# One transformer encoder layer on eight cores: the first loads put in another order, with two waits

## The chip, the cores and the metric

The kernel runs on the 8 cores of one Trainium2 chip, each core on one batch element. The metric is the device time of the slowest core, in microseconds (us); lower is better. Below, PE or TensorE is the matmul engine, DVE or VectorE, ACT or ScalarE and POOL or GpSimd are the three others that compute, and SP only issues DMAs.

## The reference, cut to what matters

```python
def hybrid_layer(x, mem, ...):                       # x (8, 2048, 1024) f32
    proj = x @ w_in                                  # 5376 columns
    glu_in, q, k, v, q_mem, gate_logits = split(proj)
    y_conv = conformer_conv(glu_in, ...)             # a * sigmoid(g), depthwise conv of 31, LayerNorm, silu, @ w_conv_out
    y_attn = windowed_gqa(q, k, v, rel_bias, attn_sink) @ w_attn_out     # +-128 tokens, T5 bias, sink per head
    y_mem = memory_attention(q_mem, mem, w_mem_kv) @ w_mem_out
    gates = sigmoid(gate_logits + b_gate)
    merged = gates[0] * y_conv + gates[1] * y_attn + gates[2] * y_mem
    x = layer_norm(ALPHA * x + merged @ w_o)
    gate, up = split(x @ w_ffn_in)
    return layer_norm(ALPHA * x + (silu(gate) * up) @ w_ffn_out)
```

## The kernel before

Each core computes the whole layer for its 2048 tokens. The tokens are cut into four tiles of 512 (k = 0 to 3), and the GLU's 512 channels into four chunks (c = 0 to 3) with a gate half and an "a" half. One GLU group is eight matmuls of 128x128 by 128x512 into one PSUM bank. The program is one long list of instructions for each engine, written out in the order in which the Python code calls them; nothing reorders them at run time. Each engine runs its own list in order and stops at a wait.

Loads of weights and of x go out on GpSimd's queue (`load`, line 281), since they cast f32 to bf16 on the way; each has a semaphore of its own. Small constants go out on SP's queue, with one semaphore for rb33 and onehot (`t_rb`) and one for the five others, relvalid, bgate, dwsc, cvec and esink8 (`t_small`, line 279), which counts as reached when all five are there. `load_glu(c, half)` loads one block of GLU weights (128x1024; half 1 is the gate), `load_xt(k)` the two halves of x tile k (128x2048 each). In all eight blocks and two x tiles are issued at the start; then GpSimd sets up constants (identity, eps, masks, ones, pads; lines 302 to 318).

Around the start, the lists of the other engines are these:

- TensorE: gate group (tile 0, chunk 0), its first four matmuls on the first x half and the last four on the second; the "a" group of the same; the bias matmul on rb33 and onehot (`setup_bias`, line 449); gate (0, 1); a (0, 1); then the groups of tile 1 and the other chunks, sixteen groups in all. After them come the q groups, which need w_q.
- PSUM: groups of one bank take turns on four single banks (4 to 7). A bank comes free when the instruction that reads it is done: the tanh for a gate group, the multiply on VectorE for an "a" group, the exponential for the bias.
- ScalarE: first the exponential of esink8 (line 329), which waits for `t_small`; then the tanh of the first gate group (line 372), the exponential of the bias (line 452), and the other tanhs. A table load goes ahead of the first.
- VectorE: copies of the identity, two small scalings that wait for `t_small` (lines 325 and 327), the GLU multiply (line 380), the bias times relvalid (line 454).
- SP, behind its small loads: the store of the first GLU result to u_scratch, the store of the bias table to gexp_scratch, more stores of GLU results.
- GpSimd, behind its constants: the load of Brev from gexp_scratch, which waits for that store to land, and only then w_q, w_kv, w_qm, memt, w_mkv and x tiles 2 and 3.

```python
        for kc in range(8):
            tk = mm(ps[:, b, :], lhs(kc), rhs(kc), kc == 0, kc == 7,
                    [dd, deps, t_xt[k][0]] if kc == 0 else [t_xt[k][kc // 4]], inc=(kc == 7))
...
    t_esink = act.run(lambda: nc.scalar.activation(esink8[:], esink8[:], AF.Exp), [t_small])
...
        btab["st"] = load(gexp_d.ap(), geb, [t_b1], sp)
        btab["rev"] = load(Brev, bass.AP(gexp_d, 0, [[1, 128], [512, 8], [1, 384]]), [btab["st"]])
```

Of the kernel before, what the change touches and what calls it, by code (L numbers as in the profile page):

```python
# [93 lines left out]
def build_nc():  # L94
    plan = _build(None)[1]
    return _build(plan)[0]

def _build(plan):
    nc = bass.Bass("TRN2", target_bir_lowering=False)

    def din(name, shape):
        return nc.dram_tensor(name, list(shape), F32, kind="ExternalInput").ap()
# [5 lines left out]
    sinkp_d = din("sinkp", [1, 8])  # L108
    onehot_d = din("onehot", [32, 512])
    relvalid_d = din("relvalid", [1, 512])  # L110
    bgate_d = din("bgate", [128, 24])
    dwsc_d = din("dwsc", [128, 128])
    cvec_d = din("cvec", [128, 12])
# [21 lines left out]
    pool = Eng(nc, nc.gpsimd, "pool", plan)  # L135
    sp = Eng(nc, nc.sync, "sp", plan)
# [4 lines left out]
    def new_slot(name="s"):  # L141
        _slot_n[0] += 1
        return Slot(nc, f"{name}{_slot_n[0]}")

    def dma(e, out, in_, slot, deps=()):
        e.wait(deps)
        e.eng.dma_start(out=out, in_=in_).then_inc(slot.sem, 16)  # L147
        slot.count += 16
        return slot.tok()
# [3 lines left out]
    def V(kb, shape, dt=BF16, p0=0):  # L153
        esz = 2 if dt == BF16 else 4
        n = 1
        for s in shape[1:]:
            n *= s
        off = int(round(kb * KB))
        a = ARENA[p0:p0 + shape[0], off // 2: off // 2 + (n * esz) // 2]
        if dt != BF16:  # L160
            a = a.bitcast(dt)
        if len(shape) >= 3:
            names = "abcdefg"[:len(shape) - 1]
            pat = "p (" + " ".join(names) + ") -> p " + " ".join(names)
            a = a.rearrange(pat, **{nm: shape[i + 1] for i, nm in enumerate(names[:-1])})
        return a
# [4 lines left out]
    bgate = nc.alloc_sbuf_tensor("bgate_sb", [128, 24], F32)  # L171
    dwsc = nc.alloc_sbuf_tensor("dwsc_sb", [128, 128], F32)
    ident4 = nc.alloc_sbuf_tensor("ident4", [128, 32], F32)
    cvec = nc.alloc_sbuf_tensor("cvec_sb", [128, 12], F32)
    esink8 = nc.alloc_sbuf_tensor("esink8", [128, 8], F32)
# [91 lines left out]
    rv = V(145, [8, 512], F32)  # L267
# [4 lines left out]
    s_bias, s_small = new_slot("bias"), new_slot("small")  # L272
    dma(sp, rb33[:], rbp_d, s_bias)
    t_rb = dma(sp, oh, onehot_d, s_bias)
    dma(sp, rv, relvalid_d.partition_broadcast(8).rearrange("p a b -> p (a b)"), s_small)
    dma(sp, bgate[:], bgate_d, s_small)
    dma(sp, dwsc[:], dwsc_d, s_small)
    dma(sp, cvec[:], cvec_d, s_small)
    t_small = dma(sp, esink8[:], sinkp_d.partition_broadcast(128).rearrange("p a b -> p (a b)"), s_small)

    def load(out, in_, deps=(), e=None, name="ld"):
        return dma(e or pool, out, in_, new_slot(name), deps)

    t_glu, t_xt = {}, [[None] * 2 for _ in range(4)]

    def load_glu(c, half=None):
        for i in ((1, 0) if half is None else (half,)):
            t_glu[c, i] = load(wglu[:, c, i], w_glu_d[:, c, i])

    def load_xt(k):  # L290
        for h in range(2):
            t_xt[k][h] = load(xT[:, k, 4 * h:4 * h + 4, :], xt_d[:, k, 4 * h:4 * h + 4, :])

    load_glu(0, 1)
    load_xt(0)
    load_glu(0, 0)
    load_glu(1)
    load_xt(1)
    load_glu(2)
    load_glu(3)  # L300

    t_idz = pool.run(lambda: nc.gpsimd.memset(ident_f[:], 0.0))
    t_identf = pool.run(lambda: nc.gpsimd.affine_select(
        out=ident_f[:], in_=ident_f[:], pattern=[[-1, 128]], compare_op=ALU.not_equal,
# [11 lines left out]
    t_pads = pool.run(lambda: nc.gpsimd.memset(U0[:, :, T + 32:UW], 0.0))  # L316
    t_vones = pool.run(lambda: nc.gpsimd.memset(vaug[:, :, :, 64:65], 1.0))
    t_vm1 = pool.run(lambda: nc.gpsimd.memset(vm129[:, :, :, 128:129], 1.0))

    t_ident = dve.run(lambda: nc.vector.tensor_copy(ident_bf[:], ident_f[:]), [t_identf])  # L320
    for r in range(4):
# [1333 lines left out]
```

How the kernel before makes its waits and increments, by code:

```python
    def wait(self, deps):  # L45
        for tok in _flat(deps):
            if tok[0] == "E":
                _, src, v = tok
                k = id(src)
                if self.seen.get(k, 0) >= v:
                    continue
                self.seen[k] = v
                src.needed.add(v)
                if self.plan is not None:
                    self.eng.wait_ge(src.sem, src.vmap[v])
            else:
                sem, val = tok
                k = id(sem)
                if self.seen.get(k, 0) >= val:
                    continue
                self.eng.wait_ge(sem, val)
                self.seen[k] = val
# [1 line left out]
    def run(self, fn, deps=(), inc=True):  # L64
        self.wait(deps)
        ins = fn()
        if inc:
            self.v += 1
            if self.plan is None or self.v in self.plan[self.name]:
                ins.then_inc(self.sem, 1)
                self.real += 1
                self.vmap[self.v] = self.real
            return ("E", self, self.v)
        return None
# [70 lines left out]
    def dma(e, out, in_, slot, deps=()):  # L145
        e.wait(deps)
        e.eng.dma_start(out=out, in_=in_).then_inc(slot.sem, 16)
        slot.count += 16
        return slot.tok()
```

## Time and profile before

| | |
|---|---|
| time, median of 3 runs | 977.96 us (977.52 to 982.31) |
| the profiled execution's own time | 978.9 us |
| its span, first to last instruction, slowest core (7) | 977.9 us |
| spans of the eight cores | 970.8 to 977.9 us |
| busy on that core: PE, DVE, ACT, POOL | 96%, 63%, 45%, 30% |

The profile shows one execution. Its span runs from the first to the last instruction of the slowest core, and all times of a row count from the start of that span. "Idle before" is what an engine stood still just ahead of an instruction, and the arrow names what ended it. For a DMA the issue (on an engine's queue, SPq or POOL) and the landing are two different times.

### The profile page before, as it was taken

Reading aid. Unit: us, or ns where it says so; the run is one execution under the profiler, and the core shown is the slowest. Engines: PE = TensorE matmul, PEld = TensorE weight load, DVE = VectorE, ACT = ScalarE, POOL = GpSimd, SP = SyncE. Lnnn points to the kernel's source line nnn. Section 1 sums busy time; section 2 is a strip of 40 time slices with the busy share of each in tenths; the row PEclk is TensorE's granted clock in tenths of the full one; section 3 lists DMA queues with packets and bytes.
Section 4 is the critical chain, followed back from the end, with each engine's and each line's share of the span. In section 5 each row is a group of like instructions: output and inputs, shape, how many; then the busy total and the mean of one; then the engine's idle time right before and its main releaser. Section 6 shows DMA issues by size and latency. Waiting matters only on the chain.

```text
span 977.9 us, 16532 instructions; the slowest of 8 cores (970.8 to 977.9 us)
## 1 busy us (share of the span) xinstructions
PE 941.3 (96%) x5556; PEld 441.9 (45%) x5556; DVE 613.6 (63%) x997; ACT 438.9 (45%) x709; POOL 291.7 (30%) x296
## 2 busy tenths in 40 slices
PE   3999999999999999999999999999999999999997
PEld 1454544554444444444445444444444444444444
DVE  0323476667766857566668798876476666663555
ACT  1125657576663354444544455554122444443212
POOL 3200000112135334334321344444433233334331
PEclk9999999999999999999999999999999999999999
DMA  8898023374258999512486365665433323220232
GB/s 131 153 178 165 24 77 101 64 149 72 45 86 121 117 150 132 76 65 57 95 252 266 87 166 148 161 147 126 158 129 129 108 86 109 86 87 1 86 108 87
DMA packets 39683, 112.12 MB, mean 115 GB/s; under 512 B 4976, under 2 KB 16888, under 8 KB 38608
## 3 DMA queue, kind: packets, MB, share of 16 engines
q0 software_dynamic: 11104, 41.16, 29.0%
q1 hardware_dynamic: 28496, 69.91, 22.3%
q8 instruction: 46, 0.75, 0.3%
q14 instruction: 37, 0.30, 0.1%
HBM read 132.49 MB, written 30.47 MB: 167 GB/s over the span
## 4 chain that ended last, share of the span: by engine, by line
PE 83%; DMA 6%; DVE 5%; issue 3%; ACT 3%; SPq 0%; DVEq 0%; POOL 0%; ACTq 0%; POOLq 0%
PE ps L233 81%; DMA esink<-sinkp 2%; DMA arena<-w_q 2%; DMA arena<-w_bf_cache 1%; DMA gexp_scratch<-arena 1%; ACT arena L597 1%; ACT arena L645 1%; PE ps L1270 1%; DVE arena L1318 1%; DVE arena L1206 1%; DVE arena L1202 0%; DVE arena L807 0%; SPq L147 0%; DVE arena L806 0%; DVE arena L590 0%
## 5 line engine op out<-in xcount | busy, mean ns | idle before, releaser
L233 PE MATMUL ps<-arena 128*128 128x512 bf16 (+5 forms) x5146 | 925.7, 357 | 28.3 <-DMA arena<-xt 16.3
L233 PEld LDWEIGHTS ps<-arena 128*128 128x128 bf16 (+1 forms) x5146 | 421.9, 98 | 515.1 <-issue 69.0
L1315 ACT COPY arena<-ps 128x512 f32<-128x512 f32 x132 | 76.6, 586 | 137.3 <-PE ps L233 137.2
L1325 POOL TENSOR_TENSOR arena<-arena 128x512 bf16<-128x512 f32 x66 | 89.2, 1351 | 151.9 <-DVE arena L1318 143.8
L1318 DVE TENSOR_TENSOR arena<-arena,ps 128x512 f32<-128x512 f32 x132 | 88.0, 684 | 40.3 <-PE ps L233 39.4
L940 POOL TENSOR_TENSOR arena<-arena 128x512 f32<-128x512 f32 (+1 forms) x48 | 63.9, 1339 | 104.2 <-DVE arena L931 104.2
L1184 ACT ACTIVATE arena<-arena 128x1024 bf16<-128x1024 f32 x31 | 32.7, 1056 | 80.7 <-DVE arena L1474 69.8
L931 DVE SCALAR_TENSOR_TENSOR arena<-arena,ps 128x512 f32<-128x512 f32 x72 | 49.2, 684 | 23.9 <-ACT arena L927 18.0
L147 POOL DMA_DIRECT2D arena<-w_g x21 | 11.3, 545 | 168.4 <-PE ps L233 167.2
L923 DVE TENSOR_TENSOR arena<-arena,ps 128x512 f32<-128x512 f32 x54 | 37.1, 686 | 35.2 <-ACT arena L920 19.7
L1206 DVE SCALAR_TENSOR_TENSOR arena<-arena,rs 128x1024 bf16<-128x1024 f32 (+2 forms) x33 | 56.5, 1716 | 1.6
L920 ACT COPY arena<-ps 128x512 f32<-128x512 f32 x54 | 31.6, 585 | 55.8 <-PE ps L233 55.8
L927 ACT ACTIVATE arena<-arena,bgate_sb 128x512 f32<-128x512 f32 x54 | 39.0, 723 | 31.6 <-DVE arena L923 31.6
L645 ACT ACTIVATE arena<-ps 128x1024 bf16<-128x1024 f32 x46 | 46.6, 1025 | 13.3 <-PE ps L233 13.0
L648 DVE TENSOR_TENSOR arena<-arena 128x1024 bf16<-128x1024 bf16 x46 | 34.0, 740 | 28.8 <-ACT arena L645 28.7
L807 DVE TENSOR_TENSOR arena<-arena 128x512 bf16<-128x512 bf16 x53 | 46.7, 881 | 5.5
L1211 POOL TENSOR_TENSOR arena<-arena 128x1024 f32<-128x1024 f32 x16 | 39.9, 2501 | 30.0 <-ACT arena L1210 30.0
L1321 ACT ACTIVATE arena<-arena 128x512 f32<-128x512 f32 x66 | 41.8, 633 | 3.3 <-DVE arena L1318 3.1
L1198 POOL TENSOR_TENSOR rs<-mvt,eps_t 128x1 f32<-128x1 f32 x32 | 21.2, 663 | 73.4 <-DVE mvt L1194 63.6
L1202 DVE SCALAR_TENSOR_TENSOR arena<-arena,mvt 128x1024 f32<-128x1024 f32 (+1 forms) x33 | 42.1, 1278 | 1.5 <-DVE mvt L1194 0.2
L806 DVE TENSOR_TENSOR arena<-arena 128x1024 bf16<-128x1024 bf16 x53 | 38.6, 729 | 5.5 <-DMA arena<-w_bf_cache 5.4
L1474 DVE SCALAR_TENSOR_TENSOR arena<-arena,ps 128x1024 f32<-128x1024 f32 x15 | 18.3, 1218 | 36.5 <-PE ps L233 29.2
(117 smaller groups left out, 552.3 us busy)
## 6 DMA issues: line engine op xcount, KB each, us to landing
arena<-w_bf_cache SPq DMA_DIRECT2D x44, 512.0 KB, 3.9
arena<-u_scratch SPq DMA_DIRECT2D x64, 135.0 KB, 3.2
arena<-x SPq DMA_DIRECT2D x16, 512.0 KB, 13.9
y_scratch<-arena SPq DMA_DIRECT2D x16, 512.0 KB, 4.3
arena<-y_scratch SPq DMA_DIRECT2D x16, 512.0 KB, 3.6
out<-arena SPq DMA_DIRECT2D x15, 512.0 KB, 2.6
arena<-w_f POOLq DMA_DIRECT2D x22, 256.0 KB, 5.0
arena<-w_g POOLq DMA_DIRECT2D x9, 512.0 KB, 18.5
```

What stands on the lines that cost most here:

```text
L233: return pe.run(lambda: nc.tensor.matmul(out, lhsT, rhs, start=start, stop=stop, skip_group_check=onto), deps, inc)
L645: t_p = act.run(lambda: nc.scalar.activation(flat, bank2(b), AF.Exp, scale=0.125), [tk, PTw_free[rp], btab["t"]])
L807: t2 = dve.run(lambda: nc.vector.tensor_tensor(out=S[:, 2, :], in0=B[:, 2, :], in1=S[:, 0, :], op=ALU.subtract), [t1])
L931: t_y = dve.run(lambda: nc.vector.scalar_tensor_tensor(out=buf, in0=buf, scalar=1.0, in1=ps[:, bk, :], op0=ALU.add, op1=ALU.mult), [tk, t_th])
L940: t = pool.run(lambda: nc.gpsimd.tensor_tensor(out=out, in0=acc, in1=buf, op=ALU.add), [t_acc, t_y])
L1202: return dve.run(lambda: nc.vector.scalar_tensor_tensor(out=buf, in0=buf, scalar=mvt[:, k % 4, 0:1], in1=tab, op0=ALU.subtract, op1=ALU.mu ...
L1206: return dve.run(lambda: nc.vector.scalar_tensor_tensor(out=dst, in0=buf, scalar=rs, in1=tab, op0=ALU.mult, op1=ALU.add), deps)
L1211: return pool.run(lambda: nc.gpsimd.tensor_tensor(out=buf, in0=buf, in1=tab, op=ALU.add), [t])
L1315: return act.run(lambda: nc.scalar.copy(buf, ps[:, b, :]), deps)
L1318: return dve.run(lambda: nc.vector.tensor_tensor(out=buf, in0=buf, in1=ps[:, b, :], op=ALU.add), deps)
L1321: return act.run(lambda: nc.scalar.activation(buf, src, AF.Silu), deps)
L1325: return pool.run(lambda: nc.gpsimd.tensor_tensor(out=dst, in0=up, in1=gate, op=ALU.mult), deps)
```

## The change

GpSimd issues the gate block of chunk 0 and the two halves of x tile 0, then sets up its constants, then waits until that block has landed, then issues the other seven blocks and x tile 1. SP issues rb33 and onehot as before, then waits until the first half of x tile 0 has landed, and issues its five other loads after that. No instruction of another engine is moved.

```diff
@@ -272,33 +272,28 @@
     s_bias, s_small = new_slot("bias"), new_slot("small")
     dma(sp, rb33[:], rbp_d, s_bias)
     t_rb = dma(sp, oh, onehot_d, s_bias)
+
+    def load(out, in_, deps=(), e=None, name="ld"):
+        return dma(e or pool, out, in_, new_slot(name), deps)
+
+    t_glu, t_xt = {}, [[None] * 2 for _ in range(4)]
+
+    def load_glu(c, half=None):
+        for i in ((1, 0) if half is None else (half,)):
+            t_glu[c, i] = load(wglu[:, c, i], w_glu_d[:, c, i])
+
+    def load_xt(k):
+        for h in range(2):
+            t_xt[k][h] = load(xT[:, k, 4 * h:4 * h + 4, :], xt_d[:, k, 4 * h:4 * h + 4, :])
+
+    load_glu(0, 1)
+    load_xt(0)
+    sp.wait([t_xt[0][0]])
     dma(sp, rv, relvalid_d.partition_broadcast(8).rearrange("p a b -> p (a b)"), s_small)
     dma(sp, bgate[:], bgate_d, s_small)
     dma(sp, dwsc[:], dwsc_d, s_small)
     dma(sp, cvec[:], cvec_d, s_small)
     t_small = dma(sp, esink8[:], sinkp_d.partition_broadcast(128).rearrange("p a b -> p (a b)"), s_small)
-
-    def load(out, in_, deps=(), e=None, name="ld"):
-        return dma(e or pool, out, in_, new_slot(name), deps)
-
-    t_glu, t_xt = {}, [[None] * 2 for _ in range(4)]
-
-    def load_glu(c, half=None):
-        for i in ((1, 0) if half is None else (half,)):
-            t_glu[c, i] = load(wglu[:, c, i], w_glu_d[:, c, i])
-
-    def load_xt(k):
-        for h in range(2):
-            t_xt[k][h] = load(xT[:, k, 4 * h:4 * h + 4, :], xt_d[:, k, 4 * h:4 * h + 4, :])
-
-    load_glu(0, 1)
-    load_xt(0)
-    load_glu(0, 0)
-    load_glu(1)
-    load_xt(1)
-    load_glu(2)
-    load_glu(3)
-
     t_idz = pool.run(lambda: nc.gpsimd.memset(ident_f[:], 0.0))
     t_identf = pool.run(lambda: nc.gpsimd.affine_select(
         out=ident_f[:], in_=ident_f[:], pattern=[[-1, 128]], compare_op=ALU.not_equal,
@@ -316,6 +311,13 @@
     t_pads = pool.run(lambda: nc.gpsimd.memset(U0[:, :, T + 32:UW], 0.0))
     t_vones = pool.run(lambda: nc.gpsimd.memset(vaug[:, :, :, 64:65], 1.0))
     t_vm1 = pool.run(lambda: nc.gpsimd.memset(vm129[:, :, :, 128:129], 1.0))
+
+    pool.wait([t_glu[0, 1]])
+    load_glu(0, 0)
+    load_glu(1)
+    load_xt(1)
+    load_glu(2)
+    load_glu(3)
 
     t_ident = dve.run(lambda: nc.vector.tensor_copy(ident_bf[:], ident_f[:]), [t_identf])
     for r in range(4):
```

On GpSimd the start of its list before (after four constants of the framework), where the names are the tiles written and read, and arena is the large SBUF buffer:

```order
L147 DMA arena<-w_glu 128x1024 [waits barrier_Pool_Activation_PE_DVE_SP_gather]
L147 DMA arena<-xt 128x2048 x2
L147 DMA arena<-w_glu 128x1024 x3
L147 DMA arena<-xt 128x2048 x2
L147 DMA arena<-w_glu 128x1024 x4
L302 MEMSET ident_f 128x128
L303 AFFINE_SELECT ident_f<-ident_f 128x128 [waits sem_pool]
```

And now, from the ninth of its constants on; dq_ld3 is the semaphore of the first block, dq_ld34 that of the gexp store:

```order
L309 MEMSET ones_bf 128x128
L310 MEMSET arena 128x4x32
L311 MEMSET arena 128x4x16
L312 MEMSET arena 128x32
L313 MEMSET arena 128x8
L147 DMA arena<-w_glu 128x1024 [waits dq_ld3]
L147 DMA arena<-w_glu 128x1024 x2
L147 DMA arena<-xt 128x2048 x2
L147 DMA arena<-w_glu 128x1024 x4
L147 DMA arena<-gexp_scratch 128x8x384 [waits dq_ld34]
```

The constants now stand behind the first block and x tile 0 and ahead of the seven other blocks and x tile 1; the first of these blocks carries a wait for the block issued first.

On SP the start of its list, where dq_ld4 is the semaphore of the first half of x tile 0:

```order
 L147 DMA rb<-rbp 32x8 [waits barrier_Pool_Activation_PE_DVE_SP_release]
 L147 DMA arena<-onehot 32x512
-L147 DMA arena<-relvalid 8x512
+L147 DMA arena<-relvalid 8x512 [waits dq_ld4]
 L147 DMA bgate_sb<-bgate 128x24
 L147 DMA dwsc_sb<-dwsc 128x128
```

Nothing is moved on SP; the third load carries a new wait, and the four loads and all stores behind it follow it.

## Rows read from the trace of the kernel before

**Rows 1.** The page's head and its busy times, slowest core:

```profile
span 977.9 us, 16532 instructions; the slowest of 8 cores (970.8 to 977.9 us)
...
PE 941.3 (96%) x5556; PEld 441.9 (45%) x5556; DVE 613.6 (63%) x997; ACT 438.9 (45%) x709; POOL 291.7 (30%) x296
```

**Rows 2.** Timeline, TensorE, core 7, 10 to 60 us: start, duration, engine, line, operation.

```profile
13.76 1.87 PE L233 MATMUL ps<-arena 128*128 128x512 bf16 x4 [13.76 <-DMA arena<-xt]
17.57 5.08 PE L233 MATMUL ps<-arena 128*128 128x512 bf16 x12 [1.95 <-DMA arena<-xt]
22.58 1.02 PE L233 MATMUL ps<-arena,rb 32*8 32x512 f32 x2
23.54 4.49 PE L233 MATMUL ps<-arena 128*128 128x512 bf16 x20
28.60 20.02 PE L233 MATMUL ps<-arena 128*128 128x512 bf16 x92 [0.57 <-DMA arena<-xt]
50.18 10.02 PE L233 MATMUL ps<-arena 128*128 128x512 bf16 x62 [1.56 <-DMA arena<-w_q]
```

**Rows 3.** Chain of waits in order of time, core 7: start, duration, what.

```profile
4.47 17.28 DMA esink<-sinkp
...
25.28 8.26 DMA gexp_scratch<-arena
...
35.05 14.99 DMA arena<-w_q
```

**Rows 4.** DMA view, 10 to 14 us: queue, packets, MB, share of 16 engines.

```profile
q0 software_dynamic: 169, 0.53, 88.9%
q1 hardware_dynamic: 169, 0.05, 9.1%
```

**Rows 5.** DMA view, 14 to 18 us.

```profile
q0 software_dynamic: 283, 0.54, 92.1%
q1 hardware_dynamic: 255, 0.02, 7.9%
```

**Rows 6.** DMA view, 4 to 18 us.

```profile
q0 software_dynamic: 715, 1.84, 93.6%
q1 hardware_dynamic: 567, 0.10, 6.9%
```

**Rows 7.** DMA view, 18 to 32 us.

```profile
q0 software_dynamic: 920, 2.19, 99.8%
```

**Rows 8.** Timeline, SP's queue and GpSimd, core 7, 0 to 26 us.

```profile
1.98 0.48 SPq L147 DMA_DIRECT2D arena<-relvalid  x1
...
4.47 1.27 SPq L147 DMA_DIRECT2D esink<-sinkp  x1
...
7.99 0.32 POOL L302 MEMSET ident_f<- 128x128 f32 x1
...
10.40 0.20 POOL L318 MEMSET arena<- 128x8 bf16 x1
```

**Rows 9.** DMA issues by line, 0 to 60 us: queue, KB, us to landing.

```profile
rb<-rbp SPq DMA_DIRECT2D x1, 1.0 KB, 1.5
```

**Rows 10.** Timeline, ScalarE, core 7, 20 to 36 us.

```profile
21.83 1.28 ACT L329 ACT_TABLE_LOAD   x1 [21.83 <-DMA esink<-sinkp]
...
23.24 0.58 ACT L372 ACTIVATE arena<-ps 128x512 f32<-128x512 f32 x1
```

**Rows 11.** Tile w_glu, 0 to 60 us (all eight), then its first load alone.

```profile
L147 POOL DMA_DIRECT2D arena<-w_glu x8: 557/606/733, 1.5 to 7.5; - x8
...
DMA to landing us min/median/max: 7.5/22.1/28.7
...
DMA to landing us min/median/max: 7.5/7.5/7.5
```

**Rows 12.** Busy time by window; the third last column is PEclk, the granted clock.

```profile
17.50:22.60 5.10, 5.03 (x13) 1.63 (x14) 0.26 (x2) 0.77 (x1) 0.00 (x0) 1.00 1.05 175
```

**Rows 13.** Timeline, TensorE, core 3, from x tile 1 on.

```profile
28.68 20.02 PE L233 MATMUL ps<-arena 128*128 128x512 bf16 x92 [2.25 <-DMA arena<-xt]
```

More of the change, by code:

```diff
@@ L274, in _build @@
     t_rb = dma(sp, oh, onehot_d, s_bias)
[L275 to L279, printed above, removed]
     def load(out, in_, deps=(), e=None, name="ld"):
@@ L295, in _build @@
     load_xt(0)
-    load_glu(0, 0)
-    load_glu(1)
-    load_xt(1)
-    load_glu(2)
-    load_glu(3)
+    sp.wait([t_xt[0][0]])
+    dma(sp, rv, relvalid_d.partition_broadcast(8).rearrange("p a b -> p (a b)"), s_small)
+    dma(sp, bgate[:], bgate_d, s_small)
+    dma(sp, dwsc[:], dwsc_d, s_small)
+    dma(sp, cvec[:], cvec_d, s_small)
+    t_small = dma(sp, esink8[:], sinkp_d.partition_broadcast(128).rearrange("p a b -> p (a b)"), s_small)
     t_idz = pool.run(lambda: nc.gpsimd.memset(ident_f[:], 0.0))
```

## Prediction

> **What bounds the kernel now.** Read the page's head first: TensorE is busy for 941.3 of 977.9 us [rows 1]. Whatever this change does, it does to the few stretches in which TensorE stands still. They lie at the start. The timeline of TensorE on core 7, the slowest, shows them [rows 2]: 13.76 us until the first half of x tile 0 is there, 1.95 until the second half, 0.57 for x tile 1, and 1.56 before 50.18 for w_q. In between, sixteen groups of eight matmuls (GLU, x tiles 0 and 1) are run without another wait. Past 50.18 TensorE is nearly always busy, so I take a shift of that point to pass whole into the end.
>
> Next, the chain of waits says why w_q is late [rows 3]. It starts with esink, the last small load of SP: issued at 4.47, landed 17.28 us later. ScalarE's first instruction waits for it; behind it come the tanh of the first gate group, the exponential of the bias, the store of gexp (25.28, 8.26 us to land), and only then may GpSimd issue the load of Brev and of w_q (35.05, 14.99 us to land). So the small loads that the change delays are the head of the chain that sets 50.18. That is the first thing to hold on to.
>
> Third, the DMA view by window shows why such small loads take so long. From 10 to 14 us GpSimd's queue q0 and SP's queue q1 each moved 169 packets [rows 4], from 14 to 18 us 283 and 255 [rows 5]: they take turns, one packet for one packet, though q1's are worth only 8 to 9% of the time. A small packet waits for a large one.
>
> **The change part by part** (times of core 7 in the profiled execution).
>
> *SP's five loads wait for the first x half.* They no longer share the engines while x tile 0 comes in. From 4 to 18 us q0 moved 1.84 MB [rows 6]; from 18 to 32 us, nearly alone, 2.19 MB [rows 7]. At the second rate the first would take 0.84 of its time. Upper bound of the gain: 16% of the 9.8 us from 4 to 13.76, 1.6 us; lower bound: q1's own 6.9% share, 0.7 us. Middle: 1.2 us, so the first half lands at about 12.6. For the second half (17.57, so 13.6 us) the same working gives 0.9 to 2.2, middle 1.6: 16.0.
>
> *The five loads land later.* The first was issued at 1.98, the last 2.5 us after it [rows 8]; now 12.6 and 15.1. Bounds for how long they then need: q1 put 567 packets through from 4 to 18 us [rows 6]; at the 64 per us of 14 to 18 us (beside w_glu's small packets) that is 8.9 us, at the 42 of 10 to 14 us (beside x's large ones) 13.4. Add 1.5 us from issue to a small load's landing in a free queue [rows 9]: 23.0 to 27.5. The far end: as long as before, 21.8 less 1.98, 19.8 us, so 32.4. The stream behind x tile 0 is now three w_glu blocks, then x tile 1, so between the two rates, 25.3; since the last ones trailed before (they landed at 21.8, not at 18), I take 26.0, against 21.8.
>
> *Who waits for them.* ScalarE waits at its first instruction, and all its work is queued behind it. From the wake at 21.83 to the end of the first tanh (23.24 plus 0.58) are 2.0 us [rows 10]; so the tanh ends at 28.0. TensorE has four single PSUM banks; two groups, the bias matmul and the second gate group fill them, and the next group (a, chunk 1) reuses the bank that this tanh frees. Before, that group began at 23.54 plus eight matmuls of 0.2245, 25.3, with the tanh done at 23.8: no wait. Now TensorE would be ready 7.8 us after the second half, at 23.8, and has to wait until 28.0: **a new stall of 4.2 us**, which the trace of before has nowhere. From that group to the end of the sixteen are 48.62 less 25.34 less the 0.57 that now is hidden, 22.7 us: 50.7 instead of 48.6.
>
> *The gexp store and w_q.* The store is issued 4.2 us later too, at 29.5. It landed in 8.26 us beside x tile 1's large packets. Bounds: 1.5 us (rows 9's small load) and 8.26; q0's last w_glu block is through at 7.5 plus 28.7, 36.2 us [rows 11], so nothing of q0 holds the store much past that. I take 6.0, near the upper end, since there is still a stream: 35.5, 2.0 us later than before. Brev and w_q follow at once: w_q at 52.0, TensorE's q groups at 52.2 instead of 50.18.
>
> *GpSimd's constants and its wait.* The constants (2.6 us, from 7.99 on [rows 8]) run while the x halves come in; nobody needs them before 23 us. The first block landed 7.5 us after its issue at 1.55 [rows 11], so GpSimd goes on at about 9.1; queued behind the wait are all further blocks, x tile 1, and later Brev and w_q. The x halves keep the engines fed until 16.0, so a block issued at 9.1 starts in time. I cost it at nothing; were that cover gone (first block past 13 us), each us would come straight on top.
>
> **Sum:** the x tile earlier by 1.6, the tanh later by 4.2, TensorE past its last early wait at 52.2 instead of 50.2: **2.0 us slower**. The profiled execution took 978.9 us, 1.0 more than its span; that becomes 980.9. The median of the runs shown is 977.96, 0.9 below the profiled execution; so I predict 980.0. The other cores' spans (970.8 at least, [rows 1]) leave core 7 the slowest.
>
> The bounds of the small loads give the range of this sum. At 23.0, the tanh ends at 25.0, x tile 1 again holds TensorE at 28.6, and w_q at about 49.0 ends the wait: 1 us faster, 977.0. At 32.4, the tanh ends at 34.4 and the sixteen groups at 57.1: 6.9 us slower, 984.9.
>
> **The rivals.**
> *TensorE's clock falls in the new stall (slower).* The 12 matmuls from 17.57 took 0.423 us each, those from 28.60 0.2176: 512 columns at 1.2 and at 2.4 GHz. The granted clock of that stretch reads 1.00 all the same [rows 12], so the level is read from the durations. Sixteen matmuls ran at the lower level after the idle start; a stall of 2.25 us on core 3 was followed by 92 at 0.2176 [rows 13]. A stall of 4.2 us lies between. If the clock falls, some 16 matmuls cost 0.2 us more each, 3.2 us: the sixteen groups end at 53.9, after w_q; 3.7 us slower, 981.7. Past 0.5% (4.9 us, about what a measurement can tell from no change) it goes if the small loads land after 27.2; at 27.5 it is 5.2 us, 983.2. The Trainium skill, "TensorE: Matmul & The Clock Gate", Part 1, says the slow clock is the default and activity releases it, which speaks for this rival; the slow start agrees. Against: x's wait of 13.8 us was three times as long.
>
> *The small loads pass quickly (faster).* If they did not take turns packet by packet, the last would land 1.5 us after 15.1, at 16.6, and hold nobody up. The bias matmul, the store and w_q would come 1.6 us earlier (w_q at 48.4), while x tile 1 still ends the sixteen groups at 48.6: 1.5 us faster, 976.5. The Trainium skill, "DMA: Bandwidth & Descriptors", section "Queues, rings and completion order", says an engine switches between queues at packets, which hold some 9 to 17 descriptors; by that the five loads' rows would go in a few turns. The trace's one for one [rows 4, 5] speaks against it.
>
> *Nothing in sum.* The loads land near 23.0, gain and delay cancel: within 1 us of 977.96.
>
> *The wait starves the queue.* The rest of the blocks comes late, x tile 1 with it: 2 to 3 us slower. The 7 us of cover speak against it.
>
> **How the numbers follow.** The forecast 0.50; clock 0.20; nothing in sum 0.17; quick loads 0.10; starved 0.03. Range 976.5 to 983.2: it takes in the quick loads' centre and the clock rival up to its dearer point; about half of the first, and the far end of the small loads, are left out, some 0.15. Faster by over 0.5% needs 4.9 us where no case has more than 1.5: 0.03. Slower by over 0.5%: half of the clock rival and the far end, 0.11. The rest, 0.86, is no change.
>
> **What would show it.** Right: first matmul at 12 to 13 us; ScalarE's table load at 25 to 27; a TensorE wait of 3 to 5 us for ScalarE's tanh after 24 matmuls and the bias; q groups from about 52. The clock: more than 16 matmuls of 0.42 us, some after that wait. Wrong: a table load before 22, no wait for ScalarE, q groups before 50.

## The result, and the profile after

The change is slower: 985.65 us (median of 5 runs, 984.80 to 987.28) against 977.52 us for the kernel before (median of 5), a ratio of 1.0083 with a 95% interval of 1.0071 to 1.0095. That is 8.1 us more, outside the predicted range of 976.5 to 983.2, whose centre was 980.0. The profiled execution took 987.28 us, the longest of the five; core 7 is again the slowest. In some executions, of the kernel before too, some cores show a lower granted clock (down to 0.81) and the time is longer (up to 1162 us); the times and ratios below leave such slow runs out.

```profile
span 986.2 us, 16534 instructions; the slowest of 8 cores (978.4 to 986.2 us)
```

TensorE's timeline on core 7 from 8 us on (start, duration, engine, line, operation; in brackets the idle time before and what ended it) answers to [rows 2]:

```profile
10.74 1.86 PE L233 MATMUL ps<-arena 128*128 128x512 bf16 x4 [10.74 <-DMA arena<-xt]
13.87 1.87 PE L233 MATMUL ps<-arena 128*128 128x512 bf16 x4 [1.26 <-DMA arena<-xt]
16.18 3.22 PE L233 MATMUL ps<-arena 128*128 128x512 bf16 x8 [0.44 <-DMA arena<-w_glu]
19.32 1.02 PE L233 MATMUL ps<-arena,rb 32*8 32x512 f32 x2
20.28 1.90 PE L233 MATMUL ps<-arena 128*128 128x512 bf16 x8
31.07 29.11 PE L233 MATMUL ps<-arena 128*128 128x512 bf16 x123 [8.89 <-ACT arena L374]
```

The first x half lands 3.0 us earlier than before on this core (10.74 against 13.76), the second 3.7. That is much more than the change gives: in the mean of the eight cores the first half comes 0.9 us earlier (10.86 against 11.76), and on cores 1, 2 and 6 it comes later than before. Then, behind 24 matmuls and the bias, TensorE stands for 8.89 us, waiting for ScalarE's first tanh (line 374 here). The waits for x tile 1 and for w_q are gone from the list: both are over by the time TensorE comes to them.

Why ScalarE is late stands in three views of the same core. First its own timeline, to be held against [rows 10]:

```profile
28.83 1.28 ACT L331 ACT_TABLE_LOAD   x1 [28.83 <-DMA esink<-sinkp]
...
30.24 0.58 ACT L374 ACTIVATE arena<-ps 128x512 f32<-128x512 f32 x1
```

Then SP's queue, against [rows 8]: the first small load, the last one, and the gexp store.

```profile
10.68 0.32 SPq L147 DMA_DIRECT2D arena<-relvalid  x1
...
12.97 0.50 SPq L147 DMA_DIRECT2D esink<-sinkp  x1
...
32.28 0.30 SPq L147 DMA_DIRECT2D gexp_scratch<-arena  x1
```

And the DMA view (queue, packets, MB, share of 16 engines), first from 8 to 14.7 us, then from 14.7 to 29:

```profile
q0 software_dynamic: 359, 1.00, 101.6%
...
q0 software_dynamic: 834, 2.04, 92.1%
q1 hardware_dynamic: 592, 0.10, 6.6%
```

SP issued the five loads from 10.68 to 12.97, but not one packet of its queue q1 appears before 14.7 us, 4.0 us after the first issue. From then on 592 packets take until 28.8, or 42 per us, beside 834 of GpSimd's queue. The last load lands 15.8 us after its issue; all five together are 0.10 MB.

The third thing to see is the granted clock (third last column of the busy time by window; PE's busy time and matmuls come first):

```profile
20.00:31.00 11.00, 2.18 (x9) 0.70 (x8) 0.33 (x3) 2.16 (x4) 0.00 (x0) 0.76 0.96 147
31.00:36.00 5.00, 4.93 (x12) 1.75 (x13) 2.39 (x4) 0.76 (x2) 0.99 (x2) 0.50 0.26 61
36.00:40.00 4.00, 4.00 (x20) 1.82 (x19) 4.00 (x5) 0.60 (x1) 4.00 (x8) 1.00 0.96 232
```

In the stall the clock falls to its lower level, 1.2 GHz (0.50), and the first 12 matmuls behind it take 4.93 us; at full clock [rows 2] 12 take 2.6.

**Where the 8 us are** (core 7). The group behind the wait starts at 31.07 where before it started at 25.34: 5.7 us. The waits for x tile 1 (0.57) and w_q (1.56) are swallowed by it, which leaves 3.6, and the half clock adds 2.3 (4.93 less 2.6): 5.9. ScalarE's first cast of a q group shows 5.7. Before and after:

```profile
52.16 0.58 ACT L352 CAST arena<-ps 128x512 bf16<-128x512 f32 x1 [4.52 <-PE ps L233]
```

```profile
57.90 0.58 ACT L354 CAST arena<-ps 128x512 bf16<-128x512 f32 x1 [2.80 <-PE ps L233]
```

The shift is still 5.73 us at 230. There, after two short waits, the clock falls a second time, where before the same waits left it at 1.00. The second wait and the clock of the stretch, first before, then after:

```profile
224.34 0.59 PE L233 MATMUL ps<-row,msk 6*128 6x512 bf16 x2 [0.70 <-ACT arena L645]
...
216.00:226.00 10.00, 8.67 (x78) 4.23 (x77) 7.38 (x28) 5.33 (x6) 1.06 (x2) 1.00 0.36 55
```

```profile
230.07 0.59 PE L233 MATMUL ps<-row,msk 6*128 6x512 bf16 x2 [0.70 <-ACT arena L647]
...
222.00:232.00 10.00, 8.67 (x75) 4.10 (x72) 7.31 (x28) 5.36 (x6) 1.06 (x2) 0.93 0.34 54
230.50:233.90 3.40, 3.40 (x9) 1.16 (x9) 3.04 (x7) 1.01 (x1) 0.00 (x0) 0.50 0.00 1
```

3.4 us at half clock cost 1.7, so some 7.4 of core 7's 8.3 us are accounted for; ScalarE's instructions keep a shift of 7.4 up to 467 us. After that a third fall of the clock, which core 7 does not have there before, takes part in the last 0.9: across it the shift of ScalarE's instructions goes from 6.5 to 8.05. (By 602 us it had dropped to 5.1; why was not followed.)

```profile
626.50:629.90 3.40, 3.40 (x14) 1.48 (x12) 3.30 (x5) 2.88 (x7) 1.58 (x3) 0.50 0.18 72
```

A dip near 230 shows on one to four cores in the profile of every version below, among them e1, e5, e6 and e8, whose times are not clear of the kernel before: it is not the change's alone, and what decides which core has it stays open.

Core 7 was the latest core before, so it shows least of the loss. In the mean of the eight cores the first cast of a q group comes at 57.44 instead of 50.02, 7.4 us later, and the span is 982.37 instead of 974.42, 8.0 longer. So over all cores nearly the whole loss stands before TensorE reaches the q groups, and what comes later, falls of the clock among it, adds some 0.5.

### The profile page after: what moved, and what is told of

The parts are those of the page before. It is cut to its first block, busy times and chain, and to the rows that moved or that the text cites. A ratio compares the mean times of both kernels' runs of the same rounds, so it can differ in the third digit from the quotient of the medians.

```text
span 986.2 us, 16534 instructions; the slowest of 8 cores (978.4 to 986.2 us)
## 1 busy us (share of the span) xinstructions
PE 946.7 (96%) x5556; PEld 443.5 (45%) x5556; DVE 616.8 (63%) x997; ACT 438.8 (44%) x709; POOL 291.5 (30%) x296
## 4 chain that ended last, share of the span: by engine, by line
PE 87%; DVE 3%; DMA 3%; issue 3%; ACT 3%; SPq 0%; DVEq 0%; POOL 0%; ACTq 0%; POOLq 0%
PE ps L233 86%; DMA esink<-sinkp 2%; DMA arena<-xt 1%; DMA arena<-w_bf_cache 1%; ACT arena L599 1%; PE ps L1272 1%; ACT arena L647 1%; DVE arena L592 0%; DVE arena L809 0%; ACT arena L602 0%; DVE arena L1208 0%; DVE arena L1204 0%; SPq L147 0%; PE ps L762 0%; DVE arena L650 0%
## 5 line engine op out<-in xcount | busy, mean ns | idle before, releaser
L650 DVE TENSOR_TENSOR arena<-arena 128x1024 bf16<-128x1024 bf16 x46 | 33.4, 728 | 29.3 <-ACT arena L647 29.2
L1213 POOL TENSOR_TENSOR arena<-arena 128x1024 f32<-128x1024 f32 x16 | 40.5, 2535 | 28.8 <-ACT arena L1212 28.7
L809 DVE TENSOR_TENSOR arena<-arena 128x512 bf16<-128x512 bf16 x53 | 43.7, 824 | 5.5
L808 DVE TENSOR_TENSOR arena<-arena 128x1024 bf16<-128x1024 bf16 x53 | 42.1, 795 | 4.6 <-DMA arena<-w_bf_cache 4.5
L1476 DVE SCALAR_TENSOR_TENSOR arena<-arena,ps 128x1024 f32<-128x1024 f32 x15 | 18.3, 1217 | 33.2 <-PE ps L233 23.8
```

The lines of the kernel that those rows point to most:

```text
L808: t1 = dve.run(lambda: nc.vector.tensor_tensor(out=S[:, 0:2, :], in0=B[:, 1:3, :], in1=B[:, 0:2, :], op=ALU.subtract), [dep])
L809: t2 = dve.run(lambda: nc.vector.tensor_tensor(out=S[:, 2, :], in0=B[:, 2, :], in1=S[:, 0, :], op=ALU.subtract), [t1])
```

## The experiments

The theory after the result: SP's wait makes the five small loads late, ScalarE stands at its first instruction until they are there, and everything else follows. The rival: GpSimd's new order and its wait (further blocks issued from 7.71 us on instead of 3.32) are what holds TensorE up. The kernel before was run beside each group of experiments; its medians there were 978.03 (e1 to e4), 978.13 (e5 to e7) and 977.98 us (e8, e9).

**e1: the change without SP's wait.**

```diff
     load_xt(0)
-    sp.wait([t_xt[0][0]])
     dma(sp, rv, ...)
```

> The change without SP's wait; GpSimd's order and wait stay. Theory S (SP's wait is the cause: the small loads land late, ScalarE's first instruction holds the first tanh, TensorE stalls and its clock falls): ScalarE's table load at 17 to 22 us, no TensorE wait for ScalarE ahead of x tile 1, 976 to 979 us. Theory G (GpSimd's order and wait are the cause): TensorE still late, 983 us or more.

Measured: 978.12 us, ratio 0.9998 (0.9986 to 1.0011). ScalarE's table load and TensorE's last early wait on core 7:

```profile
20.67 1.28 ACT L330 ACT_TABLE_LOAD   x1 [20.67 <-DMA esink<-sinkp]
...
28.78 31.52 PE L233 MATMUL ps<-arena 128*128 128x512 bf16 x169 [0.88 <-DMA arena<-xt]
```

GpSimd's order and its wait cost nothing that this measurement can tell. The rival falls.

**e2: SP's wait alone**, in the kernel before, with GpSimd's list as it was.

```diff
     load_glu(0, 1)
     load_xt(0)
+    sp.wait([t_xt[0][0]])
+    dma(sp, rv, ...)
...
     load_glu(0, 0)
```

> The kernel before with SP's wait alone; GpSimd's list as before. Theory S: table load at 26 to 30 us, a TensorE wait for the tanh of 7 to 10 us, 984 to 987 us. Theory G: 977 to 979 us.

Measured: 985.75 us, ratio 1.0082 (1.0069 to 1.0096), the whole loss. Core 7 shows the same picture:

```profile
29.48 1.28 ACT L329 ACT_TABLE_LOAD   x1 [29.48 <-DMA esink<-sinkp]
...
31.72 28.59 PE L233 MATMUL ps<-arena 128*128 128x512 bf16 x122 [9.57 <-ACT arena L372]
```

With before, e1 and the change this is a square of four: the two halves of the change add up (0.9998 and 1.0082 against 1.0083), and SP's wait is all of it within the intervals.

**e3: SP waits for the first weight block instead of x.** A dose between none and the full one.

```diff
-    sp.wait([t_xt[0][0]])
+    sp.wait([t_glu[0, 1]])
```

> The change with SP waiting for the first weight block (landed at 5.8 to 7.6 us) instead of the x half. If the five loads need a fixed number of packet turns beside GpSimd's stream, they land 1 to 3 us earlier than in the change, since more of their turns go beside the x tile's large packets: table load at 25 to 27, stall 5 to 7 us, 982 to 984 us. If their landing goes with their issue one for one, table load near 25.5, 981 to 983. If landing is set by GpSimd's stream alone, no change: 985 to 986.

Measured: 980.66 us, ratio 1.0022 (1.0013 to 1.0032). Core 7, first and last small load, table load, TensorE's wait, and the clock of the stretch behind that wait:

```profile
6.52 0.32 SPq L147 DMA_DIRECT2D arena<-relvalid  x1
...
8.63 0.69 SPq L147 DMA_DIRECT2D esink<-sinkp  x1
...
23.51 1.28 ACT L331 ACT_TABLE_LOAD   x1 [23.51 <-DMA esink<-sinkp]
...
25.75 34.43 PE L233 MATMUL ps<-arena 128*128 128x512 bf16 x152 [4.13 <-ACT arena L374]
...
25.70:31.00 5.30, 5.25 (x13) 1.90 (x14) 2.69 (x4) 0.74 (x2) 0.00 (x0) 0.50 1.06 178
```

The loads go out 4.2 us earlier than in the change and land 5.3 earlier, sooner than any of the three cases had them; one for one is the nearest. TensorE's wait is 0.7 to 4.1 us on seven cores and none on the eighth; in the change it was 6.95 to 10.05 on all. The loss is smaller with it: 0.22% against 0.83%. The wait on core 7 is almost the stall of 4.2 us that was forecast, and the clock fell in it. It also fell in or just behind the waits of 2.1 to 3.5 us on three other cores, and not behind those of 0.7 to 1.7 on the last three.

**e4: the clock kept up through the stall.** 36 matmuls on data already there, between the gate group of chunk 1 and the group that waits.

```diff
+    def warm():
+        for _ in range(36):
+            mm(ps[:, 0, :], wglu[:, 0, 1, 0, :], xT[:, 0, 0, :], True, True)
...
-    straight(g_list(0, [1]) + [run(setup_cw)] + ...
+    straight(g_list(0, [1])[:1] + [run(warm)] + g_list(0, [1])[1:] + [run(setup_cw)] + ...
```

> The change with 36 matmuls more on TensorE behind the second gate group, into a PSUM bank that nobody reads there (results unused, output unchanged); they fill some 7.8 us of the stall. It prices the fallen clock: if the clock's fall costs 2 to 3 us behind the stall, the a group starts at the same time but runs at 0.22 us a matmul, and the kernel takes 982 to 984 us. If the clock costs nothing that lasts, 985 to 986. If the matmuls themselves delay the a group, 987 or more.

Measured: 983.45 us, ratio 1.0055 (1.0042 to 1.0068). On core 7 TensorE, then the same window as above:

```profile
20.68 9.67 PE L233 MATMUL ps<-arena 128*128 128x512 bf16 x44
31.02 29.30 PE L233 MATMUL ps<-arena 128*128 128x512 bf16 x135 [0.66 <-ACT arena L374]
...
31.00:36.00 5.00, 4.98 (x24) 2.29 (x25) 4.07 (x6) 1.31 (x3) 1.66 (x3) 1.00 0.35 91
```

The group starts at the same time (31.02 against 31.07), but at full clock: 24 matmuls in 5 us instead of 12. The change is 2.2 us longer (985.65 less 983.45; 2.7 by the two ratios), about what the window said (2.3). The other 5.4 us, e4's own loss, are there with the clock kept up.

**e5 and e6: nobody waits for the small loads.** In e5 the change, in e6 the kernel before without either wait. relvalid, which the bias needs, has a semaphore of its own and goes ahead; the work on the four others, esink's exponential among it, moves behind the groups of chunks 0 and 1.

```diff
+    t_rv = dma(sp, rv, ..., new_slot("rv"))
...
-    t_bg = ...
-    t_cvec = ...
-    t_esink = act.run(lambda: nc.scalar.activation(esink8[:], esink8[:], AF.Exp), [t_small])
...
-        t_b1 = dve.run(lambda: nc.vector.tensor_tensor(out=geb, in0=ge, in1=rv, op=ALU.mult), [t_b0, t_small])
+        t_b1 = dve.run(lambda: nc.vector.tensor_tensor(out=geb, in0=ge, in1=rv, op=ALU.mult), [t_b0, t_rv])
...
-    straight(g_list(0, [1]) + [run(setup_cw)] + g_list(1, [0, 1]) + g_list(0, [2]) + ...
+    straight(g_list(0, [1]) + g_list(1, [0, 1]))
+    t_bg = ...
+    t_cvec = ...
+    t_esink = ...
+    straight([run(setup_cw)] + g_list(0, [2]) + ...
```

> The change with both waits, but nobody early waits for the small loads: relvalid goes out ahead of SP's wait on a semaphore of its own, and the instructions that need the four others (the exponential of esink, the two scalings, the conv weights) stand behind four more GLU groups on their engines. Theory S (the harm is only that ScalarE and VectorE are held at their heads): no TensorE wait for the tanh, small loads still landing at 26 to 30 us, first matmul at 10 to 12 us as in the change, TensorE then held by x tile 1 near 26; the gain of the early x tile is left over: 974 to 977 us. If the late small loads hurt in another way (x tile 1 or w_q later), 978 or more.

> The kernel before (no new wait, GpSimd's list as before) with the same reordering of ScalarE's and VectorE's early instructions and relvalid on its own semaphore. It tells what of e5_change_nobody_waits comes from the reordering alone: the gexp store no longer waits for esink, so w_q comes 1 to 2 us earlier on the cores that waited for it; x tile 0 lands as before. Theory S: 976 to 978 us, and e5_change_nobody_waits below it by 0 to 2 us. If the small loads cost the x tile nothing, both come out the same.

Measured: e5 978.08 us, ratio 1.0005 (0.9994 to 1.0016); e6 978.64 us, ratio 1.0008 (0.9996 to 1.0019). The loads are late in e5 too: on core 7 esink's goes out at 15.0 and lands 14.6 us later.

```profile
DMA to landing us min/median/max: 14.6/14.6/14.6
```

With nobody waiting, SP's wait costs nothing that shows: the loss needs both the late loads and the instructions that stand for them at the heads of ScalarE's and VectorE's lists. e5 moves both at once; that ScalarE's is the one that counts is read from the traces, where TensorE waits for its tanh. But the gain of the early x tile that was expected (e5 at 974 to 977) does not show either, and e6 lies above its own 976 to 978. One reason is that there is little of it: in the mean of the eight cores x tile 0 comes only 0.3 us earlier than before (11.49 against 11.76), and which cores get it early differs from one profile to the next. What became of a larger lead shows on core 4, first before, then e5:

```profile
12.43 1.87 PE L233 MATMUL ps<-arena 128*128 128x512 bf16 x4 [12.43 <-DMA arena<-xt]
...
27.53 3.65 PE L233 MATMUL ps<-arena 128*128 128x512 bf16 x11 [2.18 <-DMA arena<-xt]
```

```profile
10.39 1.87 PE L233 MATMUL ps<-arena 128*128 128x512 bf16 x4 [10.39 <-DMA arena<-xt]
...
27.04 33.24 PE L233 MATMUL ps<-arena 128*128 128x512 bf16 x177 [2.43 <-DMA arena<-xt]
```

It starts 2.0 us earlier and has 0.5 of that left at x tile 1; this is one core in one execution of each. On core 7 e5 waits for no x tile 1, but until 47.70 for w_q.

**e7: GpSimd's later blocks wait for the small loads.** The five loads have the engines to themselves, but for the rest of x tile 0.

```diff
-    pool.wait([t_glu[0, 1]])
+    pool.wait([t_small])
```

> The change with GpSimd's further blocks held until the small loads have landed: one look at how long the small loads take with an empty queue beside them. If they take turns one for one with GpSimd's packets, they now need only their own time: last issue at 13 us, landing by 16 to 19 (against 28.8), table load at 16 to 19. If they are slow by themselves, table load at 25 or later. The blocks come 9 us later than in the change, so TensorE waits for them: 982 to 990 us.

Measured, one execution: 983.14 us. The time is not the point (the blocks are late now, and TensorE waits 4.6 us on core 7 for one of them); the loads are. On core 7 the last issue, the table load and that wait; on core 3, the slowest, the DMA view from 13 to 17 us:

```profile
12.89 0.66 SPq L147 DMA_DIRECT2D esink<-sinkp  x1
...
15.80 1.28 ACT L331 ACT_TABLE_LOAD   x1 [15.80 <-DMA esink<-sinkp]
...
20.34 3.57 PE L233 MATMUL ps<-arena 128*128 128x512 bf16 x8 [4.61 <-DMA arena<-w_glu]
```

```profile
q1 hardware_dynamic: 592, 0.10, 15.2%
q0 software_dynamic: 20, 0.05, 6.4%
```

Almost alone, all 592 packets are through within 4 us, and on core 7 the last load lands 2.9 us after its issue. Beside the stream it took 15.8 us from its issue. So it is GpSimd's packets beside them that make the loads slow, not the loads themselves.

**e8 and e9: is the early x tile worth something once w_q and x tile 1 are out of the way?** e8 is e5 with Brev's load, which waits for the gexp store, moved behind w_q and w_kv. e9 is e8 with the blocks of chunks 2 and 3 ahead of x tile 1, and all groups of tile 0 ahead of those of tile 1.

```diff
     t_wkv = load(wkv, w_kv_d)
+    btab["rev"] = load(Brev, ...)
```

```diff
     load_glu(1)
-    load_xt(1)
     load_glu(2)
     load_glu(3)
+    load_xt(1)
...
-    straight(g_list(0, [1]) + g_list(1, [0, 1]))
+    straight(g_list(0, [1, 2, 3]))
```

> e5_change_nobody_waits with the load of Brev, which waits for the gexp store, moved on GpSimd behind w_q and w_kv. Theory S with the stream as the next bound (what the x tile gains is given back at x tile 1 and w_q): no TensorE wait for w_q on any core, the wait for x tile 1 near 27 stays: 0.5 to 1.5 us below e5, 976 to 978 us. If w_q was hidden on the slowest cores, no change: 978 to 979.

> e8_wq_ahead_of_brev with all GLU blocks loaded ahead of x tile 1, and all eight groups of tile 0 run ahead of tile 1's. If GpSimd's stream is the bound up to x tile 1, the blocks arrive as fast as TensorE uses them and only a wait for x tile 1 near 33 is left, after which 8 groups remain instead of 12: 1 to 2 us below e8, 974 to 977. If TensorE's own work is the bound by then, no change.

Measured: e8 977.32 us, ratio 0.9996 (0.9984 to 1.0008); e9 979.89 us, ratio 1.0020 (1.0010 to 1.0030). In e8 no core waits for w_q any more. Its median lies 0.7 us under that of before and inside the forecast of 976 to 978, but the interval, a gain of 1.6 us to a loss of 0.8, takes in no change. TensorE on core 7 of e8, where x tile 1 is the last early wait:

```profile
27.89 32.38 PE L233 MATMUL ps<-arena 128*128 128x512 bf16 x173 [1.37 <-DMA arena<-xt]
```

e9, forecast at 974 to 977, is slower. x tile 1 comes later still, and on cores 1 and 2 the clock falls in its waits. TensorE and one window on core 2 of e9:

```profile
33.64 1.02 PE L233 MATMUL ps<-arena 128*128 128x512 bf16 x4 [1.01 <-DMA arena<-xt]
...
37.17 23.02 PE L233 MATMUL ps<-arena 128*128 128x512 bf16 x94 [2.50 <-DMA arena<-xt]
...
37.00:43.00 6.00, 5.83 (x16) 2.12 (x17) 1.57 (x3) 0.60 (x1) 0.00 (x0) 0.55 1.00 174
```

No version that was run is clearly faster than the kernel before. The same three marks of each profile, as means of its eight cores, show how much of each result stands at the q groups:

| us | first matmul (x tile 0) | first cast of a q group | span |
|---|---|---|---|
| before | 11.76 | 50.02 | 974.42 |
| the change | 10.86 | 57.44 | 982.37 |
| e1 | 11.80 | 50.44 | 974.61 |
| e2 | 11.30 | 57.55 | 982.14 |
| e3 | 10.97 | 50.77 | 975.26 |
| e4 | 10.99 | 55.83 | 980.33 |
| e5 | 11.49 | 49.63 | 974.05 |
| e6 | 12.06 | 49.88 | 974.16 |
| e8 | 11.47 | 49.06 | 974.61 |
| e9 | 11.35 | 51.03 | 975.80 |

Each row is one execution. With SP's wait x tile 0 comes 0.3 to 0.9 us earlier than before; e4 reaches the q groups 1.6 us sooner than the change, which is the clock's part in the mean. e8 reaches them 1.0 us earlier than before, and its span has nothing of that left. Where e8 loses it again was not followed.

## Why the prediction was wrong

The steps that failed are the landing of the five loads, sized at 13.4 us from first issue to last landing where it took 18.2, and the choice that TensorE's clock stays up in the stall, where it fell. The waits of ScalarE and TensorE for these loads, and their order, were right. The small loads are the head of the chain; ScalarE stands for them at its first instruction, and TensorE at the group that needs the bank of the first tanh, behind 24 matmuls and the bias. GpSimd's part was put at nothing, and e1 measured no change. Its wait lasted 1.86 us, less than the stream in front of it covered:

```profile
7.71 1.63 POOL L147 DMA_DIRECT2D arena<-w_glu  x3 [1.86 <-DMA arena<-w_glu]
```

Term by term:

- **The landing of the five loads** (forecast 26.0, measured 28.8). Two errors of opposite sign lie in it. SP's wait ended at 10.7, not at 12.6, since x came earlier on this core than my whole range for it. That is largely the luck of core 7: in the mean of the eight cores x came 0.9 us earlier, within my 0.7 to 1.6. (The stretch from 18 to 32 us that I took for nearly alone held 205 packets of q1, 4.4% of the time, so those bounds may be a little low.) The time from the first issue to the last landing was 18.2 us, where I had 13.4. Its two terms both failed: 1.5 us, taken from a load into a free queue [rows 9], where it was 4.0 to the first packet alone; and the packet rate, which I placed between the two rates of before [rows 4, 5], where it was 42 per us, the slower of the two. The far bound, 19.8 us, was the nearest one: the same loads beside the same stream had already shown what they need.
- **The stall** (forecast 4.2, measured 8.89). 2.8 us of the 4.7 between them are the loads' later landing; 1.6 come from TensorE being ready earlier (22.2 instead of 23.8). That second part costs nothing: x's earlier arrival makes the wait longer, but does not move its end. My sum lists it beside the tanh's delay as if it offset part of it; it does not.
- **The clock.** I forecast that a stall of 4.2 us leaves the clock up and gave the other case 0.20. At 8.89 us it fell; it costs 2.2 us by e4, 2.3 by the window, where the rival had 3.2. The choice was wrong for the stall that I forecast, too: e3's wait of 4.13 us on core 7 was followed by the lower clock (0.50). The Trainium skill, "TensorE: Matmul & The Clock Gate", Part 1, on which the rival leaned, says that the slow clock is the default and activity releases it; the trace agrees, with 0.50 behind the wait. Against the rival I had put x's start of 13.8 us, which was followed by slow matmuls and spoke for it as much as against it. And I took core 3's wait of 2.25 us, after which the clock stayed up [rows 13], for the rule: on core 4 of the same trace it fell after a wait of 2.18.

```profile
28.80:32.20 3.40, 3.18 (x8) 1.21 (x8) 1.40 (x2) 0.45 (x1) 0.36 (x1) 0.50 1.05 202
```

- **The gexp store and w_q** (forecast landed 6.0 us after the issue, w_q at 52.0 as the bound). The store was issued at 32.28, and GpSimd, which waits for it, went on at 35.01, 2.7 us later: by then the stream was through.

```profile
35.01 0.92 POOL L147 DMA_DIRECT2D arena<-gexp_scratch  x1 [22.50 <-DMA gexp_scratch<-arena]
```

  w_q was in time, and the sixteen groups themselves set the end. This error made the forecast higher: of its 2.0 us, 1.5 came from this bound, and by the sixteen groups alone (50.7) the sum gave 0.5. So it brought the forecast nearer to the result by luck.
- **The sum stops at 52 us.** I let a shift pass whole into the end. On core 7 it passed whole to 230 (5.73 us), but later falls of the clock came on top, for which the sum had no term. In the mean of the eight cores all that comes after the q groups is some 0.5 of 8.0, so this step was nearly right.
- **The range.** Its upper end was a rival at a dearer point. The far bound of the loads and the clock's fall are not two cases but one: with later loads the stall is longer, and the clock fell on all cores of the change (waits of 6.95 us and more) where in e3 it stayed up on some. I had left out the far bound (984.9, before any clock). The time came out near it, but not by its sum: the loads landed at 28.8 and not at 32.4, and falls of the clock took the place of the difference. That it came so near is chance.

The rival of quick small loads is refuted by the change itself, and e7 shows why they are slow: 592 packets of q1 took 14.1 us beside 834 of q0, and under 4 us almost alone. The Trainium skill, "DMA: Bandwidth & Descriptors", section "Queues, rings and completion order", says that an engine drains a whole packet, typically 9 to 17 descriptors, before it turns to another queue; my conclusion from it, that these rows would go in a few turns, is not borne out. Whether the profile's packets are the page's packets or its descriptors no run here shows.

## What to carry to other kernels

Before a small load is put behind a wait to make room for a large one, look who stands for it at the head of an engine's list: one instruction for a constant that nobody needs until later holds up all that is queued behind it. Price small loads that are issued into a running stream by what the same loads took beside that stream before, not by a free queue. Price a new stall with the clock down, where the trace of before has the clock falling after a shorter one. And an early arrival is a gain only up to the next wait: on core 4 of e5 x tile 0 came 2.0 us sooner, and at x tile 1 0.5 was left. Before reading such a lead off one core, look at all eight.

## What the runs showed of the hardware

The first packet of SP's queue appeared 4.0 us after its issue while GpSimd's queue was moving large packets, and 2.2 us after it on core 7 of e7, where only the rest of x tile 0 was beside it; in a free queue a small load had landed after 1.5 us [rows 9]. The fall of the clock at 230 was not expected either: TensorE was busy for 8.67 of the surrounding 10 us both before and after, with the same two short waits, and only after the change did the granted clock go to 0.50 for 3.4 us. No run here tells what decides it.
